# Order of work around six norms in an fp32-accurate three-layer transformer kernel: next layer's first group by token tile, slabs split ahead, modulation slabs moved, identity load first

## The reference

```python
h = rms_norm(x, norm_g[i, 0]) * (1.0 + sc_a) + sh_a
y = moba_attention(...) if i % 2 == 0 else diff_attention(...)
x = x + g_a * rms_norm(y, norm_g[i, 1])
h = rms_norm(x, norm_g[i, 2]) * (1.0 + sc_f) + sh_f
x = x + g_f * rms_norm(swiglu_2(h, ffn_w_in[i], ffn_w_out[i]), norm_g[i, 3])
```

## Time and profile before

| | |
|---|---|
| median of 3 runs | 1032.08 us |
| profiled execution | 1029.36 us |
| its span, first to last instruction | 1027.9 us |
| around the span | 1.5 us |
| TensorE busy | 996.1 us (97%) |
| VectorE busy | 687.2 us (67%) |
| ScalarE busy | 492.6 us (48%) |
| mean granted TensorE clock | 0.987 |

### The profile page before, as it was taken

How to read it: one execution, slowest core, us unless ns; L and a number is a source line. 1 busy time by engine, 2 the same in 40 slices (tenths; PEclk the granted TensorE clock), 3 DMA queues, 4 the chain that set the end, 5 groups by cost and what they waited for, 6 DMA issues and landing times.

```text
span 1027.9 us, 16180 instructions
## 1 busy us (share of the span) xinstructions
PE 996.1 (97%) x6852; PEld 916.7 (89%) x6852; DVE 687.2 (67%) x983; ACT 492.6 (48%) x685; POOL 32.9 (3%) x51
## 2 busy tenths in 40 slices
PE   7999999989999998999989999998999989999998
PEld 6988999889998997999889999997997779999997
DVE  6766656777757676887675556557997684544443
ACT  6644433564343345565464343446666574334341
POOL 3000000000000001000000000001000010000000
PEclk9999999989999999999989999999999989999999
DMA  9943577539886875696537666663875327465501
GB/s 369 371 166 123 192 253 258 197 130 338 323 283 230 308 270 193 238 350 228 187 127 282 217 236 221 230 244 125 324 264 211 127 100 287 164 205 168 201 1 41
DMA packets 33303, 225.65 MB, mean 220 GB/s; under 512 B 3997, under 2 KB 4277, under 8 KB 6864
## 3 DMA queue, kind: packets, MB, share of 16 engines
q1 hardware_dynamic: 31104, 219.00, 59.2%
q0 software_dynamic: 1552, 4.88, 1.4%
q10 hardware_dynamic: 576, 0.74, 0.2%
HBM read 223.54 MB, written 1.08 MB: 219 GB/s over the span
## 4 chain that ended last, share of the span: by engine, by line
PE 92%; DVE 4%; ACT 2%; DMA 1%; issue 1%; ACTq 0%; POOL 0%; DVEq 0%
PE psum L568 20%; PE psum L569 20%; PE psum L570 20%; PE psum L594 9%; PE psum L595 9%; PE psum L596 9%; PE psum L748 2%; PE psum L309 1%; DVE low L498 1%; ACT work_v L340 1%; PE psum L814 1%; DMA const<-in_const 1%; ACT lam_pr L963 1%; DVE x_res L418 1%; DVE raw L507 0%
## 5 line engine op out<-in xcount | busy, mean ns | idle before, releaser
L498 DVE TENSOR_TENSOR low<-raw,high 128x2048 fp32r<-128x2048 f32 (+1 forms) x160 | 363.3, 2276 | 181.6 <-ACT high L490 181.6
L568 PE MATMUL psum<-h_hi,high 128*128 128x256 f32 x1600 | 458.9, 287 | 0.0
L569 PE MATMUL psum<-h_lo,high 128*128 128x256 f32 x1600 | 454.9, 284 | 0.0
L570 PE MATMUL psum<-h_hi,low 128*128 128x256 f32 x1600 | 454.9, 284 | 0.0
L490 ACT ACTIVATE high<-raw 128x2048 fp32r<-128x2048 f32 (+1 forms) x160 | 302.4, 1900 | 75.5 <-PE psum L596 64.3
L568 PEld LDWEIGHTS psum<-h_hi,high 128*128 128x128 f32 x1600 | 309.5, 193 | 6.3 <-issue 2.8
L569 PEld LDWEIGHTS psum<-h_lo,high 128*128 128x128 f32 x1600 | 309.5, 193 | 1.4 <-issue 0.2
L570 PEld LDWEIGHTS psum<-h_hi,low 128*128 128x128 f32 x1600 | 309.2, 193 | 0.0
L594 PE MATMUL psum<-high,y_hi 128*128 128x512 f32 x328 | 128.7, 392 | 0.0
L595 PE MATMUL psum<-low,y_hi 128*128 128x512 f32 x328 | 128.0, 390 | 0.0
L596 PE MATMUL psum<-high,y_lo 128*128 128x512 f32 x328 | 127.7, 389 | 0.0
(11 more groups left out here) (161 smaller groups left out, 755.1 us busy)
## 6 DMA issues: line engine op xcount, KB each, us to landing
raw<-in_gate_up SPq DMA_DIRECT2D x66, 1024.0 KB, 5.2
raw<-in_ada SPq DMA_DIRECT2D x48, 1024.0 KB, 6.1
raw<-in_down SPq DMA_DIRECT2D x33, 1024.0 KB, 5.8
raw<-in_mix SPq DMA_DIRECT2D x14, 1024.0 KB, 6.9
raw<-in_moba_qk SPq DMA_DIRECT2D x8, 1024.0 KB, 6.7
raw<-in_diff_qk SPq DMA_DIRECT2D x8, 1024.0 KB, 6.7
raw<-in_qk SPq DMA_DIRECT2D x4, 1024.0 KB, 15.1
raw<-in_branch SPq DMA_DIRECT2D x4, 1024.0 KB, 5.0
```

The lines of the kernel that those rows point to most:

```text
L498: nc.vector.tensor_tensor(low[n % N_LO][:, s], raw[i % N_RAW][:, s], high[n % N_HI][:, s].bitcast(F32), ALU.subtract).then_inc(*rest.up(key))
L568: nc.tensor.matmul(to, a, hi(k), start=first, stop=False)
L569: nc.tensor.matmul(to, a, lo(k), start=False, stop=False)
L570: m = nc.tensor.matmul(to, r, hi(k), start=False, stop=last and j > j0)
```

## The change

- `N_RAW, N_HI, N_LO = 6, 4, 4` becomes `N_RAW, N_HI = 8, 6`; `low[i]` is now the same memory as `raw[i]`, so a load waits until TensorE is done with the slab that had the buffer, not until it is split.
- At stages 0 to 4 the transposes of tile 0 stand between the last two groups of matmuls of the sub-layer. The output product runs its last three slabs, and the down product its last three groups, tile by tile.
- Each feed-forward layer's group 0 is computed with a token tile stationary (`pe_rows`): tile 0, then the transposes of tile 1, then tile 1; the hidden values are transposed back by four transposes (`pe_turn_rows`).
- Both attentions now begin with two value slabs on tile 0, tile 1's transposes, then tile 1.
- Splits go further ahead before a norm (FAR = 5; branch slabs AHEAD + 1 and + 2).
- The diff attention has no ada slabs; all 16 of them now lie in the feed-forward layer before it. Its apply, norm and transpose steps are rearranged.
- ScalarE's queue loads the identity first; ten instead of five blank products keep TensorE busy at the start.

```diff
-N_RAW, N_HI, N_LO = 6, 4, 4
+N_RAW, N_HI = 8, 6
...
-            if g:
+            if 0 < g < FG - 2:
                 order.append((down, base * FG + g - 1))
-        return order + [(down, base * FG + FG - 1)]
+        return order + [(down, base * FG + g) for g in range(FG - 3, FG)]
...
-            (turn2 + 4, turn3 - 2), (turn3 + 4, turn4 - 2), (turn4 + 1, turn5 - 3)]
+            (turn2 + 4, turn3 - 2), (turn3 + 3, turn3 + 16), (turn3 + 17, turn4 - 5)]
...
+            yield from square_y(0, 0)
+            yield from square_y(0, 1)
...
+            yield from square_x(0)
+            yield from square_y(1, 0)
+            for g in range(2):
+                yield from act_affine(stage, 0, g)
+            yield from square_y(1, 1)
+            yield from square_x(1)
+            for g in range(3):
+                yield from act_affine(stage, 1, g)
...
-                yield from sp.wait_ge(*((rest, b) if before == "main" else (summed, b)))
+                yield from sp.wait_ge(*((slab, b) if before == "main" else (summed, b)))
...
-            if n >= N_LO:
-                yield from dve.wait_ge(slab, n - N_LO)
...
+        FAR = AHEAD + 2
...
+            yield from pe_moving(name, [wide_part(WIDE[0])], data, ready, KC // 2, KC, freed_by_norm(stage), name, first)
+            parts = [wide_part(index) for index in WIDE[1:]]
+            turn = {(1, 0, 1): lambda: pe_turn(stage, 0)}
+            yield from pe_moving(name, parts, data, ready, KC // 2, KC, freed_by_norm(stage), name, {**second, **turn})
...
+        def pe_rows(f, t):
...
+                for k in range(KC):
+                    yield from pe.wait_ge(h_lo_made, (before, t, k))
+                    hi, lo = h_hi[:, k, tile_of(t)], h_lo[:, k, tile_of(t)]
+                    nc.tensor.matmul(to, hi, wh[:, k, :], start=a == 0 and k == 0, stop=False)
+                    nc.tensor.matmul(to, hi, wl[:, k, :], start=False, stop=False)
+                    m = nc.tensor.matmul(to, lo, wh[:, k, :], start=False, stop=a == 1 and k == KC - 1)
...
+            yield from pe_rows(f, 0)
+            yield from pe_turn(before, 1)
+            yield from pe_rows(f, 1)
+            for g in range(1, FG):
                 yield from pe_still(gate_up, base * 2 * FG + g, h_of, h_ready(before), [[(evacuated, ("silu", f, g))]])
+                if g == 1:
+                    yield from pe_turn_rows(f)
...
+                yield from act_next(*up, AHEAD if g < FG - 1 else FAR)
...
+            yield from pe_down(f, FG - 3, FG - 2, FG - 1, between=turn)
...
-                    yield from dve_next("branch", 2 * n + half)
+                    yield from dve_next("branch", 2 * n + half, AHEAD + n * (half + 1))
...
+                    if tag == "diff" and g == 3:
+                        yield from dve_apply_pairs((0, 4))
                     yield from dve_next(tag + "_qk", 4 + g)
                     yield from dve_attend(tag, 2 * g - 1)
...
                     yield from dve_attend(tag, 6)
+                    yield from dve_weigh(*dve_behind.pop(0))
+                    yield from dve_next(v, 2)
                     yield from dve_attend(tag, 7)
+                    yield from dve_apply_pairs((2, 6))
+                    yield from dve_next(v, 3)
                     yield from dve_scale_pairs(0, 2)
+                    yield from dve_turn_pairs(0, 2)
+                    yield from dve_apply_pairs((4, None), (6, None))
+                    yield from dve_scale_pairs(4, 6)
+                    yield from wide("diff_o", ({}, {0: lambda: dve_turn_pairs(4, 6)}))
...
+            nc.scalar.dma_start(ident, dram["const"][:, IDENT:IDENT + P]).then_inc(*ident_in.up("ident", by=16))
             for t in range(NT):
                 nc.scalar.dma_start(x_res[:, t, 512:], dram["x"][tile_of(t), 512:]).then_inc(*x_in[t].up("right", by=16))
```

More of the change, by code:

```diff
@@ new lines, in row_tmp @@
+        def row_tmp(t, a):
+            return work_v[:, 0, (2 * t + a) * S:(2 * t + a + 1) * S]
+        def pe_rows(f, t):
+            gate_up, _, base, before, _ = FFN[f]
+            o = yield from bank(("rows", f, t), (evacuated, ("silu row", f, t)), (produced, ("row", f, t)))
+            for a in range(2):
+                n = NUM[gate_up, base * 2 * FG + a * FG]
+                yield from pe.wait_ge(rest, n)
+                wh = high[n % N_HI][:, :].rearrange("p (k n) -> p k n", k=KC)
+                wl = low[SLOT[n]][:, :].rearrange("p (k n) -> p k n", k=KC)
+                to = o[:, a * S:(a + 1) * S]
+                for k in range(KC):
[4 more added lines that the diff above has]
+                    m = nc.tensor.matmul(to, lo, wh[:, k, :], start=False, stop=a == 1 and k == KC - 1)
+                m.then_inc(*slab.up(("row", f, t, a), *((n,) if t == NT - 1 else ())))
@@ new lines, in act_row, with dve_row @@
+        def act_row(f, t):
+            yield from act.wait_ge(slab, ("row", f, t, 1))
+            nc.scalar.activation(row_tmp(t, 0), psum[bank_of["rows", f, t]][:, 0:S], ACT.Silu).then_inc(
+                *evacuated.up(("silu row", f, t)))
+        def dve_row(f, t):
+            yield from dve.wait_ge(evacuated, ("silu row", f, t))
+            nc.vector.tensor_tensor(row_tmp(t, 1), psum[bank_of["rows", f, t]][:, S:2 * S], row_tmp(t, 0), ALU.mult).then_inc(
+                *produced.up(("row", f, t)))
@@ new lines, in dve_turn_rows @@
+        def dve_turn_rows(f):
+            yield from dve.wait_ge(hi_made, ("hidden", f, 0))
+            nc.vector.tensor_tensor(y_lo[:, 0:2, :], pair(bank_of["turned rows", f]), y_hi[:, 0:2, :].bitcast(F32), ALU.subtract).then_inc(
+                *lo_made.up(("hidden", f, 0)))
+        def pe_ffn(f, meanwhile={}):
+            gate_up, _, base, before, behind = FFN[f]
+            yield from pe_rows(f, 0)
+            yield from pe_turn(before, 1)
+            yield from pe_rows(f, 1)
+            for g in range(1, FG):
@@ L687, in dve_ffn @@
                     yield from meanwhile[g]()
-            for i in range(2):
-                yield from dve_next(down, base * FG + FG - 2 + i, AHEAD - i)
+            yield from dve_next(down, base * FG + FG - 1)
         def pool_table():
@@ L1247, in scalar @@
                         yield from act_attend(tag, 2 * g - (2 if what == "q" else 1))
+                        if tag == "diff" and g == 3 and what == "q":
+                            yield from act_apply_pairs((0, 4))
                 if tag == "moba":
```

254 lines of the change are left out of this document (109 added, 145 removed).

## The result

The changed kernel takes 1022.35 us (median of 4 runs, 1022.11 to 1022.51), the kernel before 1031.85 us on the same chip (1031.52 to 1032.9). The ratio is 0.9909, 95% interval 0.9896 to 0.9922: 9.5 us less. A second measurement of both kernels (e11) gave 0.9915 [0.9903, 0.9928].

A forecast was written before the change was run, and what follows sets the result against it. TensorE bounds the kernel, busy 996.1 of 1027.9 us, with gains in its waits and low-clock stretches. Norms -17.5, diff attention +5.9, clock +1.3, transposes +1.5, start -0.4: -9.2, from 1032.1 to 1022.9 us; range 1015 to 1029.

The forecast's parts named there:

- The norms and the work made late by the splits: Stages 0 to 4: pauses and half speed of 31.1 us shrink to 13.6 us of residue and late work, -17.5.
- The mixer's merge: Mixer output: VectorE's extra splits delay merged gates, TensorE waits 1.1, 1.7 and 1.4 us, sum 4.2; bounds 0 to 6.
- The diff attention: Diff attention: TensorE waits for probabilities and remainders sum to 8.4 us, 5.9 more than before; bounds -2.4 to +9.
- turn 7: Diff attention: transposing head 7's probabilities, wanted at 32.5 but weighed only at 35.9, makes TensorE wait 3.5 us.
- Tile 0's turn: Norms: tile 0's transposes need 5.8 us, two groups of 12 matmuls cover 5.45 us; 0.3 us left over.
- The end of the first feed-forward layer: Before stage 1: hidden values ready after 11.5 us, wanted at 11.2; 0.7 us with the norm, loads cost 0.
- The start: Kernel start: identity loaded first ends a 3.83 us wait, but x and other loads come little before it; -0.4 us.
- The clock: Diff attention: 3.5 us pause, nearer 3.92 (a fall) than 2.58 (none), brings one clock fall, 1.3 us.
- The transposes back: Three feed-forward layers: four transposes of 0.11 us and their latency in each cost 1.5 us.
- Rival A: Mixer output and diff attention: VectorE has more slack, late work does not come; 1010.0 down to 1007.6 us; chance 0.30.
- Rival B: Norms, stages 0 to 4: clock falls all the same, 17 us lost, 1040; chance 0.08, with late loads 0.11.
- Rival C: Each stage: last-group transposes themselves wait 2 us or more, gain eaten to within 0.2%; chance 0.06.

The follow-up runs named there:

- e11: The changed kernel, unchanged, measured once more beside the others on the same chip; 1022.6 us, ratio 0.9915 to the kernel before.
- e5: Changed kernel with group 0 of each feed-forward layer as before: both tiles together, tile 1's transposes ahead, no transposes back; 1041.42 us, ratio 1.0098 to the kernel before.
- e10: Changed kernel with tile 0's transposes behind the last matmul of the sub-layer at stages 0 to 4; 1033.52 us, ratio 1.0019 to the kernel before.
- e2: Changed kernel with the mixer's branch slabs split as late as before (AHEAD alone); 1026.36 us, ratio 0.9945 to the kernel before.
- e3: Changed kernel with diff attention reordered: VectorE splits between a pair's copy and join, ScalarE splits before squaring; same work; 1019.51 us, ratio 0.9879 to the kernel before.
- e8: Changed kernel with one extra split at branch slab 2, none at 3, and one split less in the output products; 1022.91 us, ratio 0.9917 to the kernel before.
- e12: The kernel before, unchanged, profiled once more in a single look; 1033.27 us, span 1031.8.
- e4: Changed kernel with eight of the sixteen ada slabs back in the diff attention; 1028.53 us, ratio 0.9962 to the kernel before.
- e9: Changed kernel with old start, reordered diff attention, fewer splits ahead before the merge, stage 0 and stage 1; 1012.82 us, ratio 0.9813 to the kernel before.
- e7: Changed kernel with one slab less split ahead at the end of the feed-forward layers (FAR - 1); 1022.54 us, ratio 0.9911 to the kernel before.

## Why the prediction was right, and where its steps were not

The forecast was -9.2 us and 1022.9 us; measured are -9.5 and 1022.35. The mechanism was right; that the number agrees to 0.3 us is in part luck, as the end of this list shows.

- **The norms and the work made late by the splits** (31.1 us before, 13.6 after, -17.5): 31.2 to 14.2, -17.0; by stages 6.3, 2.6, 2.4, 1.55 and 1.35 us where the forecast had 5.5, 1.7, 2.8, 1.7 and 1.9. Shown from both sides, by the losses counted from matmul starts and by e5 and e10, which take its two parts out.
- **The mixer's merge** (1.1 + 1.7 + 1.4): idle 1.01, 1.28, 1.02, with the latency around each 4.1 us in all. e2 shows the cause. What the step did not say is that removing the splits there would cost more.
- **The diff attention** (waits 1.45, 0.6, 3.5, 2.15 us, one fall): 1.38, 0.44, 2.48, 1.67, one fall. A loss of 8.8 us in place of the 9.7 of the sum. The mis-sized term is turn 7. e3 shows that the cause was the order: VectorE idle between a pair's copy and join.
- **Tile 0's turn** (0.3 us left over): at stages 0 and 2 it was 0.85 and 0.94. I had priced the chain of the norm and its cover, but not the splits that VectorE does ahead of the norm; e2, where four stand there, makes it 3.17 us, and e8, with one less, brings it to 0.35 and 0.
- **The end of the first feed-forward layer** (0.3 to 0.4 us for hidden group 10): 1.17 us, and up to 3 us in other runs. The step that failed is "with 3 slabs split ahead and one in use 4 loads can be under way ... 0". On average over a layer that holds, but with FAR = 5 a split asks for the fifth slab ahead, whose load starts only when its buffer comes free. e3's rows show ScalarE waiting for it. The view of ScalarE's waits of the changed kernel shows loads as a releaser of its rounds in many places, the longest sum for gate and up slabs:

```profile
ACT high L490 <- DMA raw<-in_gate_up: 27.9, 18, 5.1
```

  Before, one round waited for a load, 1.4 us. Of TensorE's waits only the one ahead of stage 1 is shown to come from them; those at the merge and at turn 7 are the same to 0.05 us in all profiles with the same order there, however late the loads were. The 0 that the forecast gave to the loads left out this one place.
- **The start** (-0.4): of the wrong sign, by the timelines +0.5 to +1.1 against e12, and +2.1 against the profile that the forecast was made from. "x, the column constants and the first half slab come only little before it" took x's arrival for fixed; the load that is put ahead of it moves it.
- **The clock** ("2.58 us, without a fall, and 3.92 us, with one"): the bound between the two was no rule. The fall I took for a pause of 3.5 us came behind one of 2.48, and e12 has one behind 2.58. The place was right, and steadily so (eight of nine profiles with that pause have the fall); the reason given for it, that 3.5 us lies nearer to 3.92 than to 2.58, was not.
- **The transposes back** (+1.5 us) and the ada slabs moved (0 outside the diff attention) left nothing in the traces that speaks against them. From the 25th matmul to the first L700 (now L766) the kernel before took 236.86 us and the changed one 236.27: 7.3 to 6.3 us lost, and some 0.45 us for one layer's transposes back. By e4 the move of the ada slabs is worth 5 us by time.

-17.0, +6.4, +1.5 and +0.5 to +1.1 make -8.6 to -8.0; with the +2.1 of the first profile's start, -7.0, as the two spans differ (1027.9 and 1021.0). The medians differ by 9.5. What is missing lies in the kernel before: most of its other executions are longer than that profile (e12 by 3.9 us, with one fall more), which the forecast knew as 2.7 us between profile and median and took for the same in both kernels. In the changed kernel profile and median agree (1022.51 and 1022.35; the forecast's profiled execution was 1020.2). So the errors of the steps, +0.5, -0.8 and +0.9 to +2.5, and this one went against each other.

**Rival A** (VectorE has slack): the waits came, and e4 and e2 show that VectorE's order has none to give at these two places. But e9 comes to 1012.82 us, near A's 1010.0, with the same work on VectorE: the slack was there by load, and only another order could use it. **Rival B** (the clock falls at norms): refuted by the windows at 1.00 in all five places, with waits of up to 1.3 us around them. The Trainium skill (TensorE: Matmul & The Clock Gate, "A second HAM failure mode: psum-queue depth-cycling") tells of another kernel, in which frequent micro-idles between groups of matmuls made the clock swing between its two levels. Here pauses of 0.3 to 1.7 us did not, neither in the changed kernel nor in e9; where it fell between the start and the end, it began in or behind a pause of 1.99 us or more, in every kernel of this study. **Rival C** (the transposes wait themselves): 0.9 us at two stages, nothing at the others.

## What to carry to other kernels

A chain of latencies between two layers is hidden by giving TensorE independent work on half of the tokens, and both halves need it: the transposes of the first half inside the last matmuls, and a first group computed by halves for the second. Whatever is done ahead to make room is then in order with the latency-bound steps of its engine, so place it where that engine would wait anyhow (between a copy and the join that needs another engine's result), not in front of what TensorE wants next. And price a small edit at the place where its work goes, not only where it leaves: e2 and e7 removed the waits they aimed at and won nothing.

## What the hardware showed that I had not expected

- The length of a pause did not decide whether the clock fell. The same program had the same pause of 2.58 us once with TensorE at full speed behind it and once with 3.4 us at half speed (e12). At one place, the wait for hidden group 10 ahead of stage 1, e2 had a pause of 1.99 us with a fall behind it (400.3 to 403.8), and e8 one of 2.83 us with none, nor had e4 behind 2.14 us. Turn 7's pause of 2.5 us had a fall behind it in eight profiles and none in e5. The rows, of e2, of e8 and of e5, in TensorE's timeline:

```profile
399.59 0.47 PE L595 MATMUL psum<-high,y_hi 128*128 128x512 f32 x1 [1.99 <-DVE y_lo L749]
```

```profile
396.78 0.47 PE L595 MATMUL psum<-high,y_hi 128*128 128x512 f32 x1 [2.83 <-DVE y_lo L749]
```

```profile
806.42 0.30 PE L865 MATMUL psum<-const,prob 128*128 128x128 f32 x1 [2.48 <-DVE prob L856]
```

  So a fall behind a pause of 2 to 3 us is a chance to be priced, not a fact; here it is worth about 1.7 us, half of 3.4 (stage 1 of e12, with the same pause, takes 1.6 us longer than that of the first profile). No profile had a fall between the start and the end without a pause of at least 1.99 us just before or around it.
- One load of 128x128 f32, put first on ScalarE's queue, moved the first use of x, which is loaded behind it, by 1.0 to 2.4 us for the first tile and by 2.8 to 3.9 us for the second.
- The round of a slab whose load starts when its buffer comes free, and that waited for this load, began 4.8 to 7.6 us after the issue. The spacing of matmuls that this made at one place, 0.23 us without a wait, varied from 0.47 to 3.22 us between runs whose program is the same there.
